# A two-layer diffusion step: where the fifth modulation vector, the convolution and the last expert are worked out

## The reference, cut to what matters

```python
for l in range(2):                                   # everything is fp32
    sh1, sc1, g1, sh2, sc2, g2 = silu(c) @ w_mod[l] + b_mod[l]      # six vectors per stream: 0 .. 5
    h = rms_norm(x, n1) * (1 + sc1) + sh1
    q, k, v, a, b = split(h @ w_in[l])               # 512, 128, 128, 512, 512 columns
    q, k = rope(rms_norm(q)), rope(rms_norm(k))      # latent tokens only for rope
    attn = softmax(q k^T / 8) v                      # 8 heads; prompt: 128 keys, latent: 384 keys
    z = depthwise_conv31(a * sigmoid(b)) + bias      # 512 channels, 31 taps, along the tokens of a stream
    x = x + g1 * (concat(attn, silu(layer_norm(z))) @ w_out[l])
    h2 = rms_norm(x, n2) * (1 + sc2) + sh2
    experts = top-2 of the 4 in the best of 4 groups, weights from sigmoid(h2 @ w_router)
    x = x + g2 * sum over the 2 experts of  weight * ((silu(h2 @ w_gate) * (h2 @ w_up)) @ w_down)
```

## Time and profile before

| | |
|---|---|
| median of 3 runs (lowest to highest) | 1155.53 us (1153.76 to 1159.91) |
| the profiled execution | 1154.12 us, its span 1152.3 us |
| PE busy | 981.6 us (85%) |
| DVE busy | 407.6 us (35%) |
| mean DMA rate | 286 GB/s |
| mean granted clock of TensorE | 0.927 |

### The profile page before, as it was taken

One profiled execution on the slowest core, in us unless ns is written; L12 is line 12 of the kernel. 1 busy time (PEld: TensorE's weight loads), 2 busy tenths in 40 slices (PEclk: granted clock), 3 DMA queues, 4 the chain that ended last, 5 costly groups with the idle time before them and its releaser, 6 DMA issues.

```text
span 1152.3 us, 11448 instructions
## 1 busy us (share of the span) xinstructions
PE 981.6 (85%) x4234; PEld 450.8 (39%) x4234; DVE 407.6 (35%) x1076; ACT 158.4 (14%) x362; POOL 114.5 (10%) x160
## 2 busy tenths in 40 slices
PE   5999979999589898987949997999768898978890
PEld 2545435554233333333344543555423333333330
DVE  0159679444111111111053966954511111111113
ACT  1101134220000000000030023431100000000001
POOL 1001200501000000000130040050110000000001
PEclk9899979998899999999969997999779999999996
DMA  9947982369989986999973353125965999999905
GB/s 339 378 164 181 316 302 74 110 218 358 425 342 423 410 336 278 421 420 426 407 285 117 145 209 125 44 104 175 369 257 206 399 426 424 425 421 425 376 20 182
DMA packets 64664, 330.11 MB, mean 286 GB/s; under 512 B 7056, under 2 KB 9744, under 8 KB 48180
## 3 DMA queue, kind: packets, MB, share of 16 engines
q1 hardware_dynamic: 44224, 277.89, 60.4%
q0 software_dynamic: 8496, 28.68, 6.8%
q10 hardware_dynamic: 11844, 22.21, 6.3%
HBM read 306.67 MB, written 22.09 MB: 285 GB/s over the span
## 4 chain that ended last, share of the span: by engine, by line
PE 69%; DMA 15%; DVE 10%; issue 3%; ACT 2%; POOL 1%; DVEq 0%; SPq 0%; ACTq 0%; POOLq 0%
PE ps L1654 21%; PE ps L1343 15%; DMA big<-in_w_up_dram 10%; PE ps L1670 10%; PE ps L1570 7%; PE ps L1359 5%; DVE scr L1016 4%; PE ps L1396 2%; PE ps L1498 2%; DMA scr<-h_rows,slot_tok 2%; DMA scr<-expert_rows,pick_y 1%; PE ps L1638 1%; PE ps L1373 1%; DMA big<-in_w_mod_dram 1%; PE ps L1522 1%
## 5 line engine op out<-in xcount | busy, mean ns | idle before, releaser
L1654 PE MATMUL ps<-big 128*64 128x512 f32 x1024 | 242.6, 625 | 47.7 <-DMA big<-in_w_up_dram 22.5
L1016 DVE SCALAR_TENSOR_TENSOR scr<-scr,convw 128x128 f32<-128x128 f32 (+1 forms) x480 | 160.6, 410 | 0.0
L1654 PEld LDWEIGHTS ps<-big 128*64 128x64 f32 x1024 | 80.2, 144 | 185.5 <-issue 172.9
L1670 PE MATMUL ps<-big,scr 128*64 128x512 f32 x624 | 144.2, 599 | 4.6 <-DVE scr L1306 4.3
L1343 PE MATMUL ps<-big 128*128 128x512 f32 (+1 forms) x384 | 145.3, 539 | 0.0
L1315 DVE TENSOR_TENSOR scr<-ps,scr 128x256 f32<-128x256 f32 x32 | 13.6, 424 | 311.0 <-ACT scr L870 311.0
L1343 PEld LDWEIGHTS ps<-big 128*128 128x128 f32 x384 | 72.5, 190 | 69.3 <-issue 67.0
L1359 PE MATMUL ps<-big,cs_rep 128*64 128x512 f32 x320 | 79.6, 645 | 14.8 <-DMA big<-in_w_mod_dram 14.8
L1570 PE MATMUL ps<-big 128*128 128x512 f32 x192 | 84.4, 594 | 1.4 <-ACT big L735 1.4
L1670 PEld LDWEIGHTS ps<-big,scr 128*64 128x64 f32 x624 | 49.1, 138 | 87.0 <-issue 86.5
L870 ACT ACTIVATE scr<-ps 128x256 f32<-128x256 f32 x32 | 12.3, 384 | 358.7 <-PE ps L1654 358.7
(11 more groups left out here) (202 smaller groups left out, 780.6 us busy)
## 6 DMA issues: line engine op xcount, KB each, us to landing
big<-in_w_gate_dram SPq DMA_DIRECT2D x32, 2048.0 KB, 15.5
big<-in_w_up_dram SPq DMA_DIRECT2D x32, 2048.0 KB, 20.6
big<-in_w_down_dram SPq DMA_DIRECT2D x32, 2048.0 KB, 17.8
big<-in_w_mod_dram SPq DMA_DIRECT2D x23, 2048.0 KB, 16.6
big<-in_w_in_dram SPq DMA_DIRECT2D x6, 2048.0 KB, 27.4
expert_rows<-scr ACTq DMA_DIRECT2D x78, 128.0 KB, 8.0
big<-in_w_out_dram SPq DMA_DIRECT2D x4, 2048.0 KB, 17.8
expert_rows<-x ACTq DMA_DIRECT2D x1, 6656.0 KB, 35.9
```

The source lines that it names most:

```text
L1016: v.scalar_tensor_tensor(out, span, w, out, ALU.mult, ALU.add).then_inc(conv_step[part_], 1)
L1654: mm = pe.matmul(ps[b * TT:(b + 1) * TT, bank, :].rearrange("p (m n) -> p m n", m=2), tokens(k), w[:, :, k, b * HF:(b + 1) * HF], start=(k ...
L1670: mm = pe.matmul(ps[b * TT:(b + 1) * TT, bank, :], src[:, k % 2 * P + k // 2 * TT:k % 2 * P + (k // 2 + 1) * TT], w[:, k, b * SEG:(b + 1) ...
```

## The change

The change has four parts.

1. **Vector 4** is made by `vector(l, 4)`, on the two column halves, ahead of the first scores; `head_fill` is gone. In layer 1, vector 2 moves from the border to the place behind the projection, as in layer 0, and `columns` for layer 1 moves into expert 15 of layer 0.
2. **Convolution by channel blocks.** `conv_half(c, m)` takes the weights as the stationary operand and streams all three tiles (384 columns) as one operand, so z comes out channel-major; `z_transposed` and `take_zT` go. A tap covers all 384 tokens in three pieces of 128 (`by_seg`), so a layer has 124 taps. POOL copies the 15 tokens at the seam between the two latent tiles, two copies per block (`halos`), and the second tap of a block waits for them. Of the 124 taps, 92 (layer 0) come before rope(1), 12 in rope(1) and rope(2), 4 after, and 16 stand in the first four heads. In layer 0 the projection begins with the conv blocks, in layer 1 with q and k/v of tile 0.
3. **Last expert by one-hot matmuls.** A token's share of expert 15 is held as a one-hot row with the weight (`last_mark`, transposed to `last_T`); its result stays in SBUF and PE adds it by six matmuls per layer (L1824). POOL can therefore gather the picks once expert 14 and the overflow are stored. Expert 15 runs differently: down of 14 first, then its overflow, then gate and up.
4. **Border and end.** From layer 0 to 1, the gathered rows are weighted and summed by PE as well (`gate_diag`, L1819, 12 matmuls of 128x512), and DVE does two operations per tile (`add_last`). At the end of layer 1, ACT and DVE add the picks as before (`add_picked`), ahead of `add_last`. The down weights of expert 14 are loaded before gate and up of 15, and block 0 of layer 1's projection is loaded after the picks have landed.

```diff
-PROMPT_TAPS = [16, 23]
-ROPE_AT = [1, 3, 5]
-ROPE_TAPS = 6
-LATE_TAPS = 4
-HEAD_TAPS = [3, 3, 3, 3, 3, 3, 3]
+EARLY_TAPS, ROPE_TAPS, BETWEEN_TAPS, LATE_TAPS, HEAD_TAPS = 80, 6, 6, 4, 4
...
+                    if l and m == 0:
+                        sp.wait_ge(picked[TILES - 1], l * 32)
...
+                def halos():
+                    for m in range(CM):
+                        pool.wait_ge(z_ready, l * CM + m + 1)
+                        g.tensor_copy(zT[:, m, 0:PAD], zT[:, m, SEG_W + P:SEG_W + P + PAD]).then_inc(halo_ready, 1)
+                        g.tensor_copy(zT[:, m, SEG_W + PAD + P:2 * SEG_W], zT[:, m, PAD:2 * PAD]).then_inc(halo_ready, 1)
...
+                        if n == 1:
+                            dve.wait_ge(halo_ready, (l * CM + m + 1) * 2)
+                        span = by_seg(zT[:, m, :])[:, :, k:k + P]
+                        out = by_seg(acc[:, m, :])
...
+                            dve.wait_ge(conv_step[m], l * TAPS + n)
+                            v.scalar_tensor_tensor(out, span, w, out, ALU.mult, ALU.add).then_inc(conv_step[m], 1)
...
+                def conv_half(c, m):
+                    s = slot_of(("in", l, c))
+                    loaded(("in", l, c))
+                    mm = accumulate(by_seg(ps[:, BLOCK_BANK[m] + c, 0:CAP]),
+                                    lambda k: slot_w(s)[:, k, m * P:(m + 1) * P], lambda k: hT_all[:, :, k, :], KD)
...
+                vector(l, 4)
                 pe.wait_ge(qkT_ready, l * 4 + 4)
...
-                    head_fill(l, hd)
...
+                    if e == E - 1:
+                        down_main(e - 1)
+                        if l + 1 < LAYERS:
+                            pe.wait_ge(y_taken, l * E + e)
+                            columns(l + 1, 0)
+                            columns(l + 1, 1)
...
+                for t in range(TILES):
+                    if border:
+                        pe.wait_ge(picked[t], (l + 1) * 32)
+                        for n in range(2):
+                            for b in range(2):
+                                pe.matmul(ps[:, 2 * FIN[t] + b, :], gate_diag[:, 2 * t + n, :],
+                                          pick_buf[t][n][:, b * SEG:(b + 1) * SEG], start=(n == 0), stop=False)
+                    if t == 0:
+                        pe.wait_ge(y_taken, (l + 1) * E)
+                    for b in range(2):
+                        mm = pe.matmul(ps[:, 2 * FIN[t] + b, :], last_T[b * TT:(b + 1) * TT, t, :],
+                                       ybuf[b * TT:(b + 1) * TT, 1, :], start=not border, stop=True)
+                    mm.then_inc(fin_ps, 1)
```

More of the change, by code:

```diff
@@ L41 @@
 MOE_SLOTS = 8
-TAKES = [0, 1, 2, 3, 8, 9, 5]
+TAKES = [0, 1, 2, 3, 4, 5]
+IN_ORDER = [[0, 1, 2, 3], [2, 3, 0, 1]]
 def loads(l):
     vec = [("v", l, j, b) for j in range(6) for b in range(2)]
-    proj, out = [("in", l, m) for m in range(4)], [("out", l, n) for n in range(2)]
+    proj, out = [("in", l, m) for m in IN_ORDER[l]], [("out", l, n) for n in range(2)]
     if l == 0:
@@ L58, in loads @@
     experts = [("g", l, 0), ("u", l, 0)]
-    for e in range(1, E):
+    for e in range(1, E - 1):
         experts += [("g", l, e), ("u", l, e), ("d", l, e - 1)]
-    return items, experts + [("d", l, E - 1)]
+    return items, experts + [("d", l, E - 2), ("g", l, E - 1), ("u", l, E - 1), ("d", l, E - 1)]
 def place():
@@ new lines, in _ @@
+                if l == 0:
+                    for t in range(TILES):
+                        first_sum(t)
+                    for t in range(TILES):
+                        first_hT(t)
+                else:
+                    first_sum(0)
+                    first_sum(1)
+                    first_hT(0)
+                    first_hT(1)
+                    first_sum(2)
+                    queries(0)
+                    first_hT(2)
+                    keys_values(0)
+                ln_loads(l)
@@ L1081, in rope @@
                     v.tensor_tensor(kk, tmp[:, 0, QW:QW + KVW], tmp[:, 1, QW:QW + KVW], ALU.add).then_inc(rope_ready, 1)
[L1083 to L1086 removed]
+                if l:
+                    rope(0)
+                dve.wait_ge(convw_ps, l + 1)
+                v.tensor_copy(convw[:, :, :].rearrange("p m k -> p (m k)"), ps[:, 1, 0:P]).then_inc(convw_ready, 1)
                 if l == 0:
[L1088 removed]
+                    v.tensor_copy(iota[:, :], ps[:, 1, P:2 * P]).then_inc(iota_ready, 1)
+                dve.wait_ge(pads_set, l * 3 + 3)
+                dve.wait_ge(convw_ready, l + 1)
+                taps(EARLY_TAPS)
+                if l == 0:
+                    rope(0)
+                    taps(BETWEEN_TAPS)
+                else:
+                    taps(BETWEEN_TAPS + ROPE_TAPS)
+                rope(1)
+                rope(2)
+                mod_take(l, 2)
+                taps(LATE_TAPS)
                 mod_take(l, 3)
[L1090 to L1091 removed]
+                mod_take(l, 4)
                 def score_max(hd):
@@ L1125, in _ @@
                         score_max(hd + 1)
-                    if hd < len(HEAD_TAPS):
-                        for n in range(HEAD_TAPS[hd]):
-                            tap(1, ROPE_TAPS + LATE_TAPS + sum(HEAD_TAPS[:hd]) + n)
+                    taps(min(HEAD_TAPS, len(CONV_ORDER) - conv_at))
                     if hd == 0:
                         score_max(1)
-                    if HEAD_FILL[hd][2] == KD:
-                        mod_take(l, HEAD_FILL[hd][0])
                     head_output(hd)
@@ L1312, in run @@
                         more_hidT()
+                    if e == E - 1:
+                        overflow(dve, n, run, ov_at)
                     dve.wait_ge(sig_ready, l * E + e + 1)
@@ L1329, in _ @@
             for t in range(TILES):
-                combine(LAYERS - 1, t)
+                add_picked(t)
+            for t in range(TILES):
+                add_last(LAYERS - 1, t)
         @block.tensor
@@ L1403, in _ @@
             columns(0, 0)
-            x_transposed(0, 0)
-            x_transposed(0, 1)
+            for t in range(TILES):
+                x_transposed(0, t)
             vector(0, 1)
@@ new lines, in _ @@
+                if l:
+                    x_transposed(l, 0)
+                    x_transposed(l, 1)
+                    project(2, 0)
+                    x_transposed(l, 2)
+                    project(3, 0)
+                for t in range(TILES):
+                    hT_first(t)
+                for m in range(CM):
+                    if m == 2:
+                        pe.wait_ge(convw_ready, l + 1)
+                        if l == 0:
+                            pe.wait_ge(iota_ready, 1)
+                    if m == 3 and l:
+                        pe.wait_ge(proj_taken, l * 6 + taken(3, 0))
+                    conv_half(0, m)
+                    if m == 0:
@@ L1471, in _ @@
                         mm.then_inc(convw_ps, 1)
-                        z_transposed(0)
-                    if i_ == 6:
-                        z_transposed(1)
-                        z_transposed(2)
-                pe.wait_ge(zT_ready, l * 3 + 3)
-                if l == 0:
-                    vector(l, 2)
+                    conv_half(1, m)
+                for c, t in QKV[2 if l else 0:]:
+                    bank = qkv_bank(l, c, t)
+                    pe.wait_ge(z_ready, l * CM + BLOCK_BANK.index(bank // 2 * 2) + 1)
+                    project(c, t)
```

443 lines of the change are left out of this document (220 added, 223 removed).

## The result

The changed kernel takes 1173.54 us, median of 4 runs (1164.62 to 1175.6); the kernel before, run beside it, 1155.41. The ratio is 1.0136, 95% interval 1.0075 to 1.0197: slower by 1.4%, where the prediction said 1119 and faster. The profiled execution took 1164.62 us, its span is 1162.8 against 1152.3.

The account below looks back on a forecast made before the run. The prediction took PE as the bound, with 69% of the last-ending chain, plus stretches where PE stands still. From 1154.1 us, -37.8 + 4.5 + 0.4 + 3.1 - 12.3 + 12.2 - 5.4 = -35.3 gave 1119; range 1106 to 1134.

Parts of the forecast that it names:

- Without them a head is 6.68 - 1.81 = 4.87.: Heads: without the two-column matmuls PE's period falls from 6.68 to 4.87 us, saving 18.9 us a layer.
- DVE under 4.87 a head: Heads: DVE needs 4.3 us per head, under PE's 4.87, and nothing from the fifth head on.
- Taps at 0.54, 0.11 more in one block: Convolution on DVE: a 384-token tap takes 0.54 us, plus 0.11 when it waits for the previous one on its block.
- The two rivals on the taps: Pieces paid singly, 0.79 us a tap, 1176 us, chance 0.05; or taps cheaper, 1105 to 1110 us, chance 0.07.
- Layer 0 up to the first maximum, +4.5: From the start to layer 0's first maximum: 4.5 us longer, at 152.2 against 147.66.
- Layer 1, +12.2: From layer 1's first transposition to its first maximum: 12.2 us longer, 118.8 against 106.6.
- Halos block: Rival: the shared-port lock delays two halo copies per block; 1123 us, or 1143 at 3 us a block; chance 0.07.
- the row above shows no such stall: GpSimd's 128x8 operation, 0.35 us beside DVE's taps, was read as no shared-port stall; the lock would cost 4 us more.
- Border, -12.3: Between the layers: 18 matmuls, 15.6 us, instead of 27.9 us before layer 1's transposes, saving 12.3 us.
- Last expert and routing, +3.5; end, -5.4: Layer 0's last expert 3.1 us and routing 0.4 us longer; the end of layer 1 5.4 us shorter.
- The experts, with their DMA, don't move as a block: Named sign of a wrong prediction; it claimed mixing, router, other experts and their DMA would move as a block.
- The heads have another limit: Rival in the heads: the loop of scores, maximum, exponential, transposes needs 5.7 us; 13 us come back, 1132 us; chance 0.13.

Follow-up runs that it names:

- experiment 5: Changed kernel with four unused matmuls per layer in PE's wait between the first scores and first transposes of the heads: 1118.29 us, ratio 0.9699.
- experiment 9: Changed kernel with two unused matmuls per layer in PE's wait for the first exponential: 1115.02 us, ratio 0.9627.
- experiment 4: Kernel before, with its fifth vector's two-column matmuls in one piece ahead of the first scores instead of in the heads: 1203.08 us, ratio 1.0401.
- experiment 10: Kernel of experiment 4 with four unused matmuls in PE's wait for the first exponential: 1178.93 us, ratio 1.0166.
- experiment 12: Changed kernel with four unused matmuls ahead of the first scores: nine runs 1150 to 1159 us, two at 1182 and 1186; ratio 0.9964 by the nine.
- experiment 6: Changed kernel with two unused matmuls in each of heads 0 to 4, none in heads 5 to 7: 1143.83 us, ratio 0.9894.
- experiment 11: Changed kernel with its fifth vector back in the heads, one k-step each, and two unused matmuls in the wait for the first exponential: 1115.59 us, ratio 0.9625.
- experiment 2: Changed kernel with one unused matmul added in each head: 1200.79 us, ratio 1.0353.

## Why the prediction was wrong, point by point

- **The step that failed: "Without them a head is 6.68 - 1.81 = 4.87."** The difference is right, 4.87 to the hundredth (experiments 5 and 9), and the stage then wins 18.5 and 19.3 us, forecast 18.9. What failed is that it was priced at a clock that the removed matmuls had themselves restored. They were not only 1.81 us of work per head, but the work that lifts PE out of the half clock into which the pause for the first exponential drops it. Without them the heads stay where they start, and are 8.93. The hint stood in the rows: the first transposes of head 0 took 0.48 in the earlier trace rows, those of a later head 0.28, behind a pause of 7.52, and the window's clock was 0.89 with PE busy. I reckoned with a cold PE in two other places and not here.
- **What stands behind the pause.** In the kernel before PE waited for DVE and ACT ahead of its first transposes just the same; the changed one even has the shorter pause (1.84 against 7.5). The change didn't make it, it took away what mended it. Experiment 4 shows that with the old kernel alone.
- **DVE under 4.87 a head:** right. 24.6 us busy in the stage, four taps in 2.6, and it leaves no wait of PE; experiment 10 shows that this matters twice.
- **Taps at 0.54, 0.11 more in one block:** measured 0.536 and 0.652. The two rivals on the taps are out, singly paid (0.79) and cheap (0.40).
- **Layer 0 up to the first maximum, +4.5:** +5.6 to +6.0. **Layer 1, +12.2:** +10.0. In layer 1 the 80 taps and their additions took 46.7 us instead of 48.5, since the 1.5 us put down for the halos did not come; each of the two ropes took 8.7 instead of 8.3 (the terms of the prediction add up to 8.4). One sign of the prediction did not come either: PE waits only 5.7 us for DVE's rope in layer 1, not over 10.
- **Halos block:** the taps of block 0 started 0.12 us behind the operation before them, the group of all 240 taps had 2.3 us of idle time ahead of it in the whole kernel, so the copies cost nothing that can be seen. But they never met a tap with two inputs. They run beside the first tap of a block (`TENSOR_SCALAR`, one tensor input), and the taps with two inputs wait for them. The case of the Trainium skill (SBUF — State Buffer, section "SBUF: two separate sides"), DVE with two SBUF inputs against a GpSimd operation that reads SBUF, therefore did not come up with the copies. It did come up in the ropes, and there the prediction's "the row above shows no such stall" was a misreading. The changed kernel, a first tap and a copy, then the same 128x8 operation of GpSimd with DVE at rest and beside taps:

```profile
67.34 0.67 DVE L1080 TENSOR_SCALAR scr<-scr,convw 128x384 f32<-128x384 f32 x1
67.37 0.19 POOL L569 COPY scr<-scr 128x15 f32<-128x15 f32 x1 [18.58 <-DVE scr L1062]
...
615.82 0.19 POOL L578 TENSOR_SCALAR stat<-stat 128x8 f32<-128x8 f32 x1 [11.05 <-DVE stat L1098]
...
114.90 0.48 POOL L578 TENSOR_SCALAR stat<-stat 128x8 f32<-128x8 f32 x1 [0.16 <-DVE stat L1098]
```

It took 0.19 us alone, 0.35 beside taps of 256 and 0.48 beside taps of 384 (to the start of the next operation 0.28 alone and 0.57 beside them). The chain of three such operations took 3.3 us instead of 2.5, and DVE then waited 0.26 to 0.30 us for it in each rope, most of the 0.4 by which these were longer than forecast. That the ports are the cause fits, but no run tests it.
- **Border, -12.3:** -13.9. The picks were in time, but not by much: the gathers were issued from 567.63 to 573.86, the first 10 us before PE began on the sums (577.61), and took 7 to 8.5 us to land, so the last were there near 582, and PE came to them at 586.99. PE had no wait for picks or for weights in the border. The 18 matmuls took 14.0 us, where 15.6 had been reckoned.
- **Last expert and routing, +3.5; end, -5.4:** with warm heads +2.0 and -3.6, in the changed kernel -3.4 and -7.9. "The experts, with their DMA, don't move as a block" was named as a way to be wrong, and they don't: 5.4 and 4.3 us of the two slow stages came back behind them.
- **The rivals.** "The heads have another limit" came nearest, but by the wrong mechanism (a loop of 5.7 us) and at under a quarter of the price (13 us of 58). Reading for the clock would have given the right one: every row of a head at half clock, so a period near twice 4.87, and the other sign.

With the pause filled the kernel has the forecast's time: 1115 measured, 1119 predicted, range 1106 to 1134. What stays open: why four runs of the changed kernel reach from 1164.6 to 1175.6 (the mean clock is 0.897 in the quickest and 0.886 in the slowest; only the quickest was profiled), and when a short pause brings the clock down and when it does not (experiments 4 and 12).

The Trainium skill (TensorE: Matmul & The Clock Gate, section "Part 1: The HAM clock gate (the "warmup" mystery)") says that the low clock is the default and that activity of PE releases it. The pause and the recovery by filler agree with that; a stage in which PE is busy for 67 of 69 us and stays at 0.52 does not follow from it, and the measurement decides.

## What to carry to other kernels

Before removing filler or moving work out of a loop of short matmuls, read the clock of the stage and how its first rows compare with the later ones: if they are up to twice as long, something behind them restores the clock, and it may be what you are removing. Where PE must wait for a microsecond or two just ahead of such a loop, matmuls without use that fit into the wait cost nothing and here decided over 58 us. And if the time of one kernel falls into two groups as far apart as one stage at half clock costs, look there first.

## What the hardware did that I hadn't expected

- The same instructions, with PE busy without a gap, took 66 us at half clock (155.41 to 221.87) or 37 at full clock (155.85 to 192.74, experiment 9), depending on the state in which they began. Without filler neither went over into the other by itself: in the changed kernel and in experiments 4 and 12 no warm head came behind a cold one, and behind a warm one, where PE had no pause, no cold one (experiments 5, 6, 9 and 11).
- A single pause of PE of 1.00 us inside a warm stage ended it (experiment 10), and one of 0.92 us ahead of it did so in some executions and, by the times, not in others (experiment 12). A wait of 2.58 us at one and the same place was followed by half clock in the kernel before and by full clock in experiment 4. So a pause of 0.9 to 2.6 us can bring the clock down, but need not.
- For the way back two matmuls of 512 columns per head were enough, or eight of 128 (6.71), and one was not (10.72) while scores stood between; in the last head, without scores, one did it (values of 1.92 and 2.05 us, experiment 2).
- A pair of 64 x 512 matmuls into the two halves of the output rows costs 5.87 - 4.87 = 1.00 us a head, the same two one after the other into one half 6.73 - 4.87 = 1.86.
